# A Fourier branch computed for tokens 0 to 128 only, the mirrored tokens taken as a sum and a difference on VectorE

## The reference

```python
def fnet_mixer(u):                       # u: (1, 256 tokens, 256 columns) of the projection
    b, s, _ = u.shape
    uf = u.astype(jnp.float32).reshape(b, s, FNET_GROUPS, FNET_GROUP_DIM)   # 4 groups of 64
    y = jnp.fft.fft2(uf, axes=(1, 3), norm='ortho').real
    return y.reshape(b, s, FNET_GROUPS * FNET_GROUP_DIM).astype(u.dtype)
```

## Time and profile before

| what | value |
|---|---|
| median of three runs | 1237.12 us |
| lowest and highest | 1236.67 and 1237.5 us |
| span of the profiled execution | 1235.1 us |
| TensorE matmul busy | 1227.5 us (99%) |
| VectorE busy | 852.4 us (69%) |
| ScalarE busy | 690.6 us (56%) |
| TensorE's granted clock | 1.000 of full speed |

### The profile page before, as it was taken

The page is one execution under the profiler, slowest core; times in us unless marked ns, Lnnn a source line. Parts: engine busy times, 40 slices in busy tenths (PEclk is TensorE's granted clock), DMA queues, the critical chain, the costliest instruction groups (busy, mean ns, idle before and its releaser), DMA issues.

```text
span 1235.1 us, 22033 instructions
## 1 busy us (share of the span) xinstructions
PE 1227.5 (99%) x9196; PEld 1151.3 (93%) x9196; DVE 852.4 (69%) x1203; ACT 690.6 (56%) x1148; POOL 38.6 (3%) x88
## 2 busy tenths in 40 slices
PE   8999999999999999999999999999999999999998
PEld 8999989988899989999999998899899999999987
DVE  6997767654476778987766554658679986665543
ACT  5897665543367664872644443567555834544432
POOL 2100100000000000110100000000000100000000
PEclk9999999999999999999999999999999999999999
DMA  9642535555535333423555555444343425555552
GB/s 358 244 168 104 192 136 189 201 205 180 195 137 183 129 132 137 171 103 124 211 184 200 187 195 197 171 151 157 114 160 141 167 103 175 176 197 188 190 203 102
DMA packets 30611, 211.77 MB, mean 171 GB/s; under 512 B 3376, under 2 KB 3760, under 8 KB 5552
## 3 DMA queue, kind: packets, MB, share of 16 engines
q1 hardware_dynamic: 30224, 210.22, 47.8%
q10 hardware_dynamic: 288, 0.14, 0.0%
HBM read 209.29 MB, written 1.05 MB: 170 GB/s over the span
## 4 chain that ended last, share of the span: by engine, by line
PE 95%; ACT 2%; DVE 1%; issue 1%; DMA 1%; SPq 0%; DVEq 0%; ACTq 0%
PE bank L548 92%; PE bank L667 1%; PE bank L900 1%; ACT w_hi L1173 1%; DMA ring<-weight_pieces 1%; DVE x_lo L1803 0%; ACT W L1489 0%; ACT W L1173 0%; SPq L1060 0%; ACT W L1460 0%; ACT mem_hi L1173 0%; ACT W L1455 0%; DVE W L1648 0%; ACT L1489 0%; ACT L1465 0%
## 5 line engine op out<-in xcount | busy, mean ns | idle before, releaser
L1684 DVE TENSOR_TENSOR w_lo<-ring,w_hi 128x2048 fp32r<-128x2048 f32 (+1 forms) x180 | 409.0, 2272 | 239.1 <-ACT w_hi L1173 238.5
L1173 ACT ACTIVATE w_hi<-ring 128x1024 fp32r<-128x1024 f32 (+1 forms) x368 | 366.5, 1047 | 238.2 <-PE bank L548 221.6
L548 PE MATMUL bank<-x_hi,w_hi 128*128 128x256 f32 x1840 | 260.0, 280 | 2.1 <-issue 1.1
L548 PE MATMUL bank<-x_hi,w_lo 128*128 128x256 f32 x1840 | 252.4, 276 | 0.0
L548 PE MATMUL bank<-x_lo,w_hi 128*128 128x256 f32 x1840 | 247.3, 277 | 0.2
L548 PEld LDWEIGHTS bank<-x_hi,w_hi 128*128 128x128 f32 x1840 | 230.6, 188 | 5.5 <-ACT x_hi L1173 2.0
L548 PEld LDWEIGHTS bank<-x_hi,w_lo 128*128 128x128 f32 x1840 | 229.0, 188 | 0.3
L548 PEld LDWEIGHTS bank<-x_lo,w_hi 128*128 128x128 f32 x1840 | 226.6, 188 | 0.6 <-DVE x_lo L1803 0.6
L548 PE MATMUL bank<-W 128*128 128x128 f32 (+4 forms) x720 | 110.1, 326 | 1.5 <-DVE W L1709 1.2
L548 PEld LDWEIGHTS bank<-W 128*128 128x128 f32 (+3 forms) x720 | 87.7, 187 | 14.2 <-issue 5.1
L548 PE MATMUL bank<-w_hi,hid_hi 128*128 128x512 f32 x304 | 76.6, 389 | 0.0
(11 more groups left out here) (265 smaller groups left out, 1218.2 us busy)
## 6 DMA issues: line engine op xcount, KB each, us to landing
ring<-weight_pieces SPq DMA_DIRECT2D x191, 1024.0 KB, 4.8
const<-constants SPq DMA_DIRECT2D x1, 1376.5 KB, 12.2
W<-x_features SPq DMA_DIRECT2D x4, 256.0 KB, 5.4
ring<-weight_pieces SPq DMA_DIRECT2D x2, 512.0 KB, 6.2
h<-x SPq DMA_DIRECT2D x2, 512.0 KB, 6.3
W<-rg_weights SPq DMA_DIRECT2D x1, 1024.0 KB, 11.2
xs<-mem_features SPq DMA_DIRECT2D x1, 1024.0 KB, 12.6
oT<-mem SPq DMA_DIRECT2D x1, 1024.0 KB, 14.3
```

The lines of the kernel that those rows point to most:

```text
L548: return nc.tensor.matmul(out, lhsT, rhs, start=first, stop=last)
L1173: return nc.scalar.activation(out, in_, ACT.Copy, scale=scale)
L1684: v.tensor_tensor(whole(w_lo, q), rows, whole(w_hi, q).bitcast(F32), ALU.subtract).then_inc(s_weight_low, 1)
```

## The change

The Fourier step along the tokens is computed for tokens 0 to 128 alone. Cosine and sine products no longer share a bank: `fyc` takes the cosine products with 129 moving columns for each column tile, `fy` the sine products with 128. ScalarE copies the 2 x 129 columns of `fyc` to `oT`. A new step `("fnet", l, 2)`, placed in VectorE's order right behind gate 0, writes tokens 255 down to 129 as cosine minus sine, with a step of -1 in the output, and then adds the sine part to tokens 1 to 127 in place. Its second instruction is what drains `fy`. The number of products stays at 8 in each layer (16 instructions). Group "m" has one fill more in each layer.

```diff
-                   [[("bnorm", l, 0), c[1]], ..., [("bturn", l), hg, ("fnet", l, 1)], [gates[0]],
+                   [[("bnorm", l, 0), c[1]], ..., [("bturn", l), hg, ("fnet", l, 1)], [gates[0], dve(("fnet", l, 2))],
...
-                    bank = fill(f"fy{l}", "m")
-                    for ft in range(2):
-                        for st in range(TT):
-                            mm(bank[:, ft * S:(ft + 1) * S], ab[:, st, ft, 0:P], dc[:, st, :], st == 0, False)
-                            ins = mm(bank[:, ft * S:(ft + 1) * S], ab[:, st, ft, P:2 * P], ds[:, st, :], False, st == TT - 1)
-                    full(ins, f"fy{l}")
+                    for name, half, wave, n in ((f"fyc{l}", 0, dc, P + 1), (f"fy{l}", 1, ds, P)):
+                        bank = fill(name, "m")
+                        for ft in range(2):
+                            for st in range(TT):
+                                ins = mm(bank[:, ft * S:ft * S + n], ab[:, st, ft, half * P:(half + 1) * P], wave[:, st, 0:n], st == 0, st == TT - 1)
+                        full(ins, name)
...
-                    drains(copy(oT[:, 2:4, :], bank2(wait_filled(act, f"fy{l}"))), f"fy{l}")
+                    drains(copy(oT[:, 2:4, 0:P + 1], bank2(wait_filled(act, f"fyc{l}"))[:, :, 0:P + 1]), f"fyc{l}")
...
+                elif kind == "fnet" and step[2] == 2:
+
+                    l = step[1]
+                    wait_drained(dve, f"fyc{l}")
+                    even, odd = oT[:, 2:4, 1:P], bank2(wait_filled(dve, f"fy{l}"))[:, :, 1:P]
+                    v.tensor_tensor(oT[:, 2:4, S - 1:P:-1], even, odd, ALU.subtract)
+                    drains(v.tensor_tensor(even, even, odd, ALU.add), f"fy{l}")
```

More of the change, by code:

```diff
@@ L436, in build @@
             attend([(f"mla{l}", n) for n in range(4)] + [(f"diff{l}", n) for n in range(4)],
-                   [[("bnorm", l, 0), c[1]], [("bnorm", l, 1), e[0]], [("bnorm", l, 2), pe(e[1]), ("high", hg[-1]), dve(e[1]), ("low", hg[-1]), ("fnet", l, 0), act(e[1])], [("bturn", l), hg, ("fnet", l, 1)], [gates[0]],
+                   [[("bnorm", l, 0), c[1]], [("bnorm", l, 1), e[0]], [("bnorm", l, 2), pe(e[1]), ("high", hg[-1]), dve(e[1]), ("low", hg[-1]), ("fnet", l, 0), act(e[1])], [("bturn", l), hg, ("fnet", l, 1)], [gates[0], dve(("fnet", l, 2))],
                     [("scan", l, 0), gates[1]], [("scan", l, 1), gates[2]], [("scan", l, 2), gates[3]], [("scan", l, 3), gates[4]],
```

## The result

The changed kernel takes 1241.14 us (median of five runs, 1239.1 to 1243.45) against 1236.7 us for the kernel before (five runs, 1236.39 to 1237.5). The ratio is 1.0035, 95% interval 1.0024 to 1.0046: slower by 4.4 us. The forecast was 1237.6 us, in a range of 1235.9 to 1239.2 us, with 86% on a difference of less than 0.2% either way. The time lies above the range, and the difference is 0.35%.

The account below looks back on a forecast made before the run. The prediction took TensorE's order to bound the kernel. Gains of 3.52 us against stalls of 1.97 + 2.00 = 3.97 us gave +0.45 us on 1237.12, so 1237.6 us, range 1235.9 to 1239.2 us.

Parts of the forecast that it names:

- What bounds the kernel: Whole kernel: TensorE's order bounds it, busy 1227.5 of 1235.1 us; any wait of TensorE adds its length.
- Part 1, the gain: Fourier step on TensorE: narrower matmuls take 1.78 instead of 3.54 us, gaining 1.76 us in each layer.
- the bound with 0.1 us for a second bank: Fourier step: lower bound of the gain if opening a second bank loses 0.1 us, 1.66 us.
- Part 2, the fills that cost nothing: ScalarE's shorter copy gains nothing; with one fill more, the first four fills behind it wait at no cost.
- Part 3, the bank of diff1 b: Before diff1's scores TensorE waits for VectorE's second new instruction to drain fy: 1.97 and 2.00 us in the two layers.
- The dearer estimate: VectorE's reversed output at the skill's slower figure: 0.37 us more in each layer, forecast 0.7 us higher.
- The sum: Whole kernel: gains 3.52 us against stalls 3.97 us, +0.45 us, so 1237.6 us; chance 86%.
- Theory A: From the experiments: TensorE's 2 us idle time at the bank makes its clock fall; wait and clock together eat the gain.
- this rival: Behind each 2 us stall TensorE's clock falls, losing up to 1.83 us each time: 1241.2 us; chance 5%.
- The sign for the clock: In the profile after, matmuls behind the idle time slower than 0.12 us each would mean the clock.
- The rival of no stall: The bank is free when diff1 is opened, so the gain stands alone: 1233.6 us; chance 7%.
- Narrow matmuls no faster: Fourier step: narrow matmuls gain nothing and both stalls are paid for nothing: 1241.1 us; chance 2%.

Follow-up runs that it names:

- The runs with 1.25 and 1.37 us: Changed kernel with one extra product inside the wait, 1238.57 us; changed kernel with VectorE's new step between w_lo of gate 1 and gate 0, 1237.2 us.
- the first run: Changed kernel with VectorE's new step placed ahead of gate 0 instead of behind it: 1233.42 us, ratio 0.9974.
- the longer wait: Changed kernel with VectorE's subtraction done four times instead of once: 1244.48 us, ratio 1.0064.

## Why the prediction was wrong

*What bounds the kernel:* right. The waits of TensorE at the bank showed in the time in every run that had them.

*Part 1, the gain:* right in mechanism and 5% too large. The step holds TensorE from 428.23 to 430.10, which is 1.87 us instead of the 1.78 forecast, and from 873.17 to 875.05 in layer 1. The gain is 1.67 and 1.66 us instead of 1.76: that this meets the bound with 0.1 us for a second bank is luck. The trace has the 16 instructions 0.11 us apart, as forecast, and no gap where the bank changes; the missing 0.09 us is behind the last one, which the next group follows after 0.20 us (0.31 us before, where the spacing was 0.22). The estimate of 107 ns a weight load, from the rule in the Trainium skill ("TensorE: Matmul & The Clock Gate", section "LDWEIGHTS (loading the stationary operand)"), agrees with the loads in the trace, which start 0.11 us apart; no run here shows whether they are what sets the pace.

*Part 2, the fills that cost nothing:* right. The only new wait of TensorE is the one at diff1. ScalarE's copy takes 0.39 us instead of 0.60.

*Part 3, the bank of diff1 b:* right, to the place and the line. Forecast 1.97 and 2.00 us, measured as idle time 1.97 and 1.98. That it agrees to a hundredth is partly luck: idle time counts from the end of the last matmul, while the forecast counted from the time at which the scores started in the trace of before (440.95). In those terms the waits are 0.36 + 1.67 = 2.03 and 0.40 + 1.66 = 2.06 us, since TensorE went on 0.14 us behind VectorE's end and not 0.05. The reversed output costs nothing: 0.41 us for each instruction, 0.33 apart. The dearer estimate, from the figure of the Trainium skill, "Vector Engine (DVE) Microarchitecture Reference", section 5.2 "Measured stream behaviour on trn2", for an output that steps by 24 words, doesn't hold for a step of -1; that page has no measurement of it.

*The sum:* this is the step that failed. It priced the wait at its length and put the clock behind it at nothing. Here the wait had that second price. I had that as a rival, with a price of 1.83 us behind each wait and a total of 1241.2 us, and gave it 5%. Measured were 1.58 and 3.14 us in the profiled execution and 1241.14 us in the median. Theory A and this rival are one and the same; that its total meets the median so closely is luck, since the losses differ by a factor of two within one execution and the runs spread over 4.4 us. The run with work inside the wait shows the sum without the clock: +0.90 us against +0.45 forecast. The two traces give +0.76 (0.36 and 0.40). So this part was a little small, by the gain and the hand-over above, and the clock's 3.5 us are what carried the time out of the range.

*Why the chance was wrong:* the evidence against the rival was one row, an idle time of 1.15 us at the start without a slow stretch behind it. The forecast wait was 1.7 times as long, and a wait longer than any in the trace is outside of what its rows can vouch for. The runs with 1.25 and 1.37 us show that one row in one execution doesn't vouch even for a tenth of a microsecond more. The price of the rival came from the first group of the kernel, slow at a granted clock of 1.00. Two windows in that group, over matmuls of one shape, show what this was:

```profile
1.50:4.50 3.00, 3.00 (x8) 2.34 (x8) 0.00 (x0) 1.49 (x2) 0.00 (x0) 1.00 0.78 215
4.70:6.20 1.50, 1.50 (x8) 1.30 (x7) 1.43 (x9) 0.86 (x2) 0.20 (x1) 1.00 0.98 369
```

Eight matmuls take 3.0 us and then 1.5 us, 0.43 us from start to start and then 0.22. The trace's first record of the clock is one of 1.00 at 4.71 us; ahead of it there is none, and the view shows 1.00 for want of one. So this place was most likely TensorE at half its clock, and the rival's price was of the right kind; the 1.00 in the view didn't speak against it.

*The sign for the clock:* it was set too low. Matmuls "slower than 0.12 us each" are there in the kernel before as well: eight of gate 0 start at 434.26 and the next eight at 435.28, 0.128 us each. Behind the wait of layer 0 it is 1.79 us for eight, 0.224 each.

*The rival of no stall:* ruled out for the changed kernel, but one move away. It needed VectorE at the step earlier; ahead of gate 0 VectorE finds its bank full and idles anyway (2.87 us before the `w_lo` at 439.30 in the earlier trace rows, 2.22 us with the step moved there). That rival's time was 1233.6 us, 3.52 under its start; measured were 1233.42 us, 3.30 under the kernel before beside it.

*Narrow matmuls no faster:* ruled out by the first run.

## What to carry to other kernels

When an edit hands the draining of a PSUM bank to another engine, count the fills to the bank's next use and find what that engine has queued ahead of the drain; the matmuls saved only bring TensorE sooner to that wait. If a wait of TensorE of over a microsecond is in the sum, give it a second price for the clock, here 1.3 to 3.1 us each, and make its chance high unless rows show the same length without a fall in many executions. Place the drain ahead of the long work on its engine, not behind it: here that alone turns 4.4 us slower into 3.3 us faster.

## What the runs showed of the hardware

TensorE's granted clock fell to 0.50 (1.2 GHz) behind idle times of 1.92 to 3.35 us that followed long full work. In the three profiles with two such waits the fall came 0.3 to 2.0 us after TensorE was back at work, and the clock then stayed low for 3.4 us in five cases and for 6.8 us in one, at the second wait of the changed kernel. The mean clock was below 1.000 in all 15 executions of the three kernels with two such waits, and in eight of eleven with one. With two waits of 1.25 to 1.39 us it was below 1.000 in about half, five of eleven and six of eleven. The mean is rounded to a thousandth. A stretch of 3.4 us at 0.50 lowers it by 0.0014 and shows as 0.999, two as 0.997; one of up to 1.2 us can hide in a 1.000. A 0.999 alone doesn't tell the place: in the profile with the step ahead of gate 0 the clock also falls at 1231.29 us, in the last microsecond of the span, and one of the 24 runs of the kernel before reads 0.999 at an ordinary 1236.58 us. In the five and six executions above the longer times go with it. Only 0.50 and 1.00 were seen where a window lay wholly in one state. By the Trainium skill, "TensorE: Matmul & The Clock Gate", section "What's actually happening", these are the gate's only two states; the trace agrees, and windows with 0.65 or 0.86 are those in which it changed.

The loss varies between executions of one program: the changed kernel spreads over 4.4 us and the longer wait over 4.6 us, where the kernel without waits spreads over 1.4 us (1232.78 to 1234.2). The five runs with wide products and the wait spread over no more than 1.4 us either (1241.91 to 1243.31), and why the loss varies stays open. A median over few runs of a kernel with such a wait can be uncertain by a microsecond or more, and a single profile can show either case.

While the clock was low, TensorE's busy time rose with it. The busy share stayed at 99% in both kernels; the place showed best in the windows' clock and in groups of the same eight instructions at 2.00 instead of 1.19 us.
